# Turning the last tile inside a unit, writing two engines' loops out, and moving one head's meta scores in a two-block kernel

## The reference

```python
for l in range(2):                                   # first block
    h = rmsnorm(x, pre_g[l])
    u_a, v_a, g_a, q, k, v, g_b = split(h @ w_in[l])
    y_a = gmlp(u_a, layernorm(v_a)) * silu(g_a)      # spatial mixing in chunks of 128
    y_b = attention(rope(rmsnorm(q)), rope(rmsnorm(k)), v) * silu(g_b)
    x = x + rmsnorm(concat(y_a, y_b) @ w_out[l], post_g[l])
h = concat(pad, meta, x)                             # second block: 16 meta tokens ahead
sb_q, sb_k, sb_v, sw_q, ... = split(rms_norm(h) @ w_in_2)
o_sb = stick_breaking_attention(sb_q, sb_k, sb_v)    # 8 heads, weights from suffix sums
o_sw = sliding_window_sink_attention(...)            # 16 heads, window of 128
merged = sigmoid(g_sb) * ((o_sb * silu(sb_z)) @ w_branch_sb) + sigmoid(g_sw) * (...)
out = rms_norm(h + merged @ w_out_2)[:, 128:]
```

## Time and profile before

| | |
|---|---|
| Time before, median of 3 runs | 984.11 us (983.71 to 984.31) |
| The profiled execution's own time | 981.8 us |
| Its span, first to last instruction | 980.0 us |
| PE busy | 961.1 us (98%) |
| VectorE busy | 639.5 us (65%) |
| ScalarE busy | 492.6 us (50%) |
| GpSimd busy | 257.1 us (26%) |
| DMA, mean | 82 GB/s |

### The profile page before, as it was taken

One profiled execution on the slowest core, in us unless ns is written; L12 is line 12 of the kernel. 1 busy time (PEld: TensorE's weight loads), 2 busy tenths in 40 slices (PEclk: granted clock), 3 DMA queues, 4 the chain that ended last, 5 costly groups with the idle time before them and its releaser, 6 DMA issues.

```text
span 980.0 us, 13699 instructions
## 1 busy us (share of the span) xinstructions
PE 961.1 (98%) x4922; PEld 812.0 (83%) x4922; DVE 639.5 (65%) x949; ACT 492.6 (50%) x903; POOL 257.1 (26%) x205
## 2 busy tenths in 40 slices
PE   7999999999999999999999999999999999999997
PEld 6988888888888888888787888888888887888885
DVE  5677777937687687846655798599557985312214
ACT  5435665624435655625347777423657983222212
POOL 2216200003126200002342010340325885224231
PEclk9999999999999999999999999999999999999999
DMA  8332201232422301132332111122320112223312
GB/s 289 109 117 71 89 22 44 62 114 87 142 87 86 105 26 44 44 129 82 108 99 77 40 43 44 43 86 87 102 92 1 44 44 81 92 89 105 129 43 86
DMA packets 66791, 80.45 MB, mean 82 GB/s; under 512 B 5520, under 2 KB 50704, under 8 KB 66720
## 3 DMA queue, kind: packets, MB, share of 16 engines
q1 hardware_dynamic: 64816, 76.64, 24.5%
q10 hardware_dynamic: 1904, 2.88, 0.9%
HBM read 77.42 MB, written 2.10 MB: 81 GB/s over the span
## 4 chain that ended last, share of the span: by engine, by line
PE 60%; issue 29%; DVE 4%; POOL 3%; ACT 3%; DMA 1%; POOLq 0%; ACTq 0%; DVEq 0%
PE ps L1944 16%; PE ps L1946 16%; PE ps L1945 16%; PE ps L2001 1%; PE ps L1999 1%; PE ps L2000 1%; PE ps L2322 1%; PE ps L2458 1%; PE ps L2473 1%; DVE pwt L1604 1%; POOL small L561 1%; DMA x<-in_x 1%; PE ps L2486 1%; PE ps L2342 1%; PE ps L2205 1%
## 5 line engine op out<-in xcount | busy, mean ns | idle before, releaser
L606 POOL TENSOR_TENSOR wlo<-raw,whi 128x2048 fp32r<-128x2048 f32 (+1 forms) x22 | 96.3, 4375 | 186.2 <-ACT whi L958 176.8
L1944 PE MATMUL ps<-whi,hhi 128*128 128x512 f32 (+1 forms) x320 | 115.9, 362 | 1.5 <-DVE hlo L1267 0.8
L1946 PE MATMUL ps<-whi,hlo 128*128 128x512 f32 (+1 forms) x320 | 114.5, 358 | 0.0
L1945 PE MATMUL ps<-wlo,hhi 128*128 128x512 f32 (+1 forms) x320 | 114.4, 357 | 0.0
L1944 PE MATMUL ps<-hhi,whi 128*128 128x512 f32 x288 | 113.6, 394 | 0.3 <-ACT sp L1055 0.3
L1946 PE MATMUL ps<-hhi,wlo 128*128 128x512 f32 x288 | 112.3, 390 | 0.0
L1945 PE MATMUL ps<-hlo,whi 128*128 128x512 f32 x288 | 112.3, 390 | 0.0
L958 ACT ACTIVATE whi<-raw 128x2048 fp32r<-128x2048 f32 (+1 forms) x29 | 53.0, 1826 | 84.0 <-PE ps L1946 74.1
L1276 DVE TENSOR_TENSOR wlo<-raw,whi 128x2048 fp32r<-128x2048 f32 (+1 forms) x29 | 63.6, 2193 | 39.4 <-ACT whi L724 38.0
L724 ACT ACTIVATE whi<-raw 128x2048 fp32r<-128x2048 f32 (+1 forms) x29 | 52.2, 1799 | 72.7 <-PE ps L1946 72.7
L1999 PE MATMUL ps<-hhi,whi 128*128 128x512 f32 x192 | 76.9, 400 | 0.0
(11 more groups left out here) (331 smaller groups left out, 2339.9 us busy)
## 6 DMA issues: line engine op xcount, KB each, us to landing
raw<-in_w_in SPq DMA_DIRECT2D x42, 1024.0 KB, 5.3
raw<-in_w_out SPq DMA_DIRECT2D x12, 1024.0 KB, 5.0
raw<-in_w_in SPq DMA_DIRECT2D x10, 512.0 KB, 4.2
raw<-in_w_branch_swa SPq DMA_DIRECT2D x4, 1024.0 KB, 5.3
raw<-in_w_branch_sb SPq DMA_DIRECT2D x4, 512.0 KB, 3.4
x<-in_x ACTq DMA_DIRECT2D x3, 512.0 KB, 6.8
out<-x SPq DMA_DIRECT2D x3, 512.0 KB, 2.6
ws<-in_spatial_w SPq DMA_DIRECT2D x2, 512.0 KB, 6.8
```

The lines of the kernel that those rows point to most:

```text
L606: pool.tensor_tensor(wlo[s][:, 0:n, :], raw[s][:, 0:n, :], whi[s][:, 0:n, :].bitcast(F32), ALU.subtract).then_inc(slab_split, 1)
L1944: pe.matmul(out_ap, lhsT=lhi(k), rhs=rhi(k), start=first and k == 0, stop=False, skip_group_check=True)
L1945: pe.matmul(out_ap, lhsT=lhi(k), rhs=rlo(k), start=False, stop=False, skip_group_check=True)
L1946: m = pe.matmul(out_ap, lhsT=llo(k), rhs=rhi(k), start=False, stop=last and k == n - 1, skip_group_check=True)
```

## The change

Five edits:

- Tile 3 is turned inside unit (0, 2), between its two groups of six products, instead of ahead of it. This holds in both layers and in the second block.
- ScalarE's and VectorE's loops over the two layers become Python loops, so the layers are written out one after the other; PE, GpSimd and SyncE keep their loops.
- At the end of a layer VectorE makes the first half of tile 2's `hlo` ahead of `normalise` of tile 3, the second half behind it.
- In the second block the meta scores of head 1 go behind both gate units, and in round 1 VectorE makes `meta_keys_lo(1)` ahead of `terms_lo(2)`.
- At the end GpSimd adds epsilon to the first half's sum as soon as that is there, and then adds this to the second half's.

```diff
-TILE_AT = {3: 2, 4: 3}
+TILE_AT = {3: 2}
+LAST_TILE_AT = 4
...
             for t in range(NT):
+                if t == 3:
+                    pool.wait_ge(fin_sq, 4)
+                    first = small2[:, 16:17]
+                    pool.tensor_tensor(first, first, eps_tile[:, 0:1], ALU.add).then_inc(last_sum, 1)
+                    pool.wait_ge(last_sum, 1)
                 pool.wait_ge(fin_sq, t + 1 + t // 3)
                 m = small2[:, 8 + t:9 + t]
-                if t == 3:
-                    pool.tensor_tensor(m, m, small2[:, 16:17], ALU.add).then_inc(last_sum, 1)
-                    pool.wait_ge(last_sum, 1)
-                pool.tensor_tensor(m, m, eps_tile[:, 0:1], ALU.add).then_inc(pool_step, 1)
+                pool.tensor_tensor(m, m, small2[:, 16:17] if t == 3 else eps_tile[:, 0:1], ALU.add)\
+                    .then_inc(pool_step, 1)
...
-            with act.Fori(0, DEPTH) as l:
+            for l in range(DEPTH):
...
-            with dve.Fori(0, DEPTH) as l:
+            for l in range(DEPTH):
...
                 normalise(l, 1, 2)
                 post_add(3)
+                transposed_x(l, 1, 2, (0,))
                 normalise(l, 1, 3)
-                transposed_x(l, 1, 2)
+                transposed_x(l, 1, 2, (1,))
...
-                    terms_lo(h + 1)
                     if h == 1:
                         meta_keys_lo(1)
+                    terms_lo(h + 1)
...
-                def by_token_half(i, half, t):
+                def by_token_half(i, half, t, turned_between=None):
...
                     for at_ in (0, 2):
+                        if at_ and turned_between is not None:
+                            x_transposed(l, 0, turned_between)
...
-                    by_token_half(i, i, t)
+                    by_token_half(i, i, t, 3 if n == LAST_TILE_AT else None)
...
             other_scores(0)
-            stick_meta_scores(1)
             gate_unit(0)
             gate_unit(1)
+            stick_meta_scores(1)
```

More of the change, by code:

```diff
@@ L2171, in tokens, with tokens_half @@
                         lambda k: whi[s][:, k, :], lambda k: wlo[s][:, k, :], KT).then_inc(unit_done, 1)
-            def tokens_half(j, half, t):
+            def tokens_half(j, half, t, turned_between=None):
                 s, tt = j % RING, slice(t * P, t * P + P)
@@ L2178, in tokens_half @@
                 for at_ in (0, 2):
+                    if at_ and turned_between is not None:
+                        x_transposed(DEPTH, 0, turned_between)
                     if (j, t) == (0, 0):
@@ L2235, in _ @@
                     m.then_inc(mt_done, 1)
-                tokens_half(j, j, t)
+                tokens_half(j, j, t, 3 if n == LAST_TILE_AT else None)
                 if t == 3:
```

## The result

The changed kernel takes 977.57 us, median of 4 runs (977.45 to 977.75); the kernel before, timed beside it, 983.91 us (983.67 to 984.31). The ratio is 0.9945, with a 95% interval of 0.9933 to 0.9956 (the two medians divide to 0.9936): 6.3 us faster, where 4.2 were forecast.

A forecast was written before the change was run, and what follows sets the result against it. TensorE, busy 961.1 of 980.0 us, was taken as the bound. The terms 1.3 + 0.75 + 1.9 + 0.27 = 4.2 us, off the median of 984.11, gave 979.9 us; range 979.0 to 982.1.

The forecast's parts named there:

- can only close gaps: Whole kernel: no matrix product is removed, so only TensorE's 18.9 us outside its busy time can be won.
- The meta scores, 1.9 us: Second block, head 1: gates fill TensorE's wait for VectorE's low part of `qsb`; 1.9 us won, bounds 0 to 2.2.
- Rival A: Meta scores of the second head: the 1.9 us are given back, 2.3 us remain, 981.8 us; chance 0.12.
- The start of the second layer, 1.3 us: Loops' back edges and turn of tile 3: unit (0,3) starts 1.3 us earlier; bounds 0.6 to 1.4.
- Rival B: Turn inside the unit fails to hide tile 3, or ScalarE and VectorE stall at the layer's start; 981.9 us, chance 0.11.
- The start of the second block, 0.75 us: Same new order without a back edge: unit (0,3) starts 0.75 us earlier; bounds 0.3 to 0.84.
- a slow first step: Start of the second block: TensorE resumes at about 474.95 with its first step 0.1 us longer; 0.2 us lost there.
- The end, 0.27 us: Behind the last product: one of three GpSimd operations is done earlier, so the root and all behind it move 0.27 us.
- The spread: Whole kernel: the forecast's own spread, from the bounds of its terms, given as 979.3 to 980.9 us.
- Rival C: ScalarE and VectorE through the second layer: fetching the second code copy shows; slower from six fetches, up to 989.7 us; chance 0.05.
- the prediction's signs of being wrong: TensorE's idle merely moved to unit (0,3) or the sums, or "issue" on ScalarE or VectorE in the second layer.

## Why the prediction was right in its parts and wrong in its sum

**The step that failed** is the last one: "That execution lies 2.3 us under the median of 984.11, so the forecast is 984.11 - 4.2 = 979.9 us." It took the 2.3 us between the profile and the timed runs for a constant that any version of the kernel carries. They were 1.7 us of half clock (983.87 - 982.2, the medians of the two groups) and chance: the profiled execution lies 0.4 us under the median of the lower group, and the 984.11 of the three runs 0.2 above that of the upper one. With it failed the premise that the change "can only close gaps": it also keeps products from running at half clock, which counts as busy time and which no list of waits shows. The clock falls behind the very stop that the change removes, so the upper group went with the stop: none of 29 runs of six kernels without it (the changed one, the meta scores alone, and the changed one without the turn, with the loops in, with the old end, with TensorE's loop out) and none of 22 with the stop filled or half filled is in an upper group. What was needed stood in the numbers: three times within 0.6 us of one another and a profiled execution 1.9 us under the lowest of them. That does not look like scatter: either every profile reads less, or something was in those three executions and not in the profiled one. A second profile would have told the two apart. And a profile at full clock can't show what a stop costs where the clock falls.

**The meta scores, 1.9 us.** Right: sums of head 1 come 540.20 - 516.78 = 23.42 us behind the last score of head 0, before 543.87 - 518.43 = 25.44, so 2.0 us; alone, the edit gives 2.0 in the lower group. The true term against the runs shown is 3.7, the rest being the clock. Rival A (the gain given back) did not come: the sums of head 0 are 2.2 us sooner and those of head 1 2.0.

**The start of the second layer, 1.3 us.** Right: from the last product of unit (1,1) to unit (0,3) it is 253.68 - 249.83 = 3.85 us, before 254.68 - 249.46 = 5.22, so 1.37. ScalarE's "issue" ahead of tile 3 is gone. Rival B's stall is what the kernel with loops in shows: there the same stretch takes 4.64 us, 0.6 less than before, which is the term's lower bound.

**The start of the second block, 0.75 us.** Right: 5.46 - 4.71 = 0.75, with a slow first step at 473.98 as foreseen. No run has this part alone.

**The end, 0.27 us.** The rows after are one GpSimd step shorter than in the kernel with the old end (0.27 us against 0.53), and the times differ by 0.2: right in the profiles, and within what five runs can tell in the times.

**The spread.** By the prediction's own bounds its ends are 984.11 - 4.7 = 979.4 and 984.11 - 3.1 = 981.0 us, not 979.3 and 980.9; nothing hangs on it.

**Rival C** (the second copy of the code fetched visibly) did not come as a cost: there are 21 packets in place of 29 on that queue, no "issue" on ScalarE at the place it named, and none of TensorE's listed waits from its back edge at 238.16 to 582.48. But one of the prediction's signs of being wrong did come: VectorE shows "issue" in the second layer, ahead of the low part of a slab, in all seven profiles with the loops out, where before the same idle ends with ScalarE's `whi`. After:

```profile
256.68 1.92 ACT L728 ACTIVATE whi<-raw 128x2048 fp32r<-128x2048 f32 x1 [1.57 <-PE ps L1951]
...
259.04 2.29 DVE L1280 TENSOR_TENSOR wlo<-raw,whi 128x2048 fp32r<-128x2048 f32 x1 [3.36 <-issue]
```

Before:

```profile
259.79 2.29 DVE L1276 TENSOR_TENSOR wlo<-raw,whi 128x2048 fp32r<-128x2048 f32 x1 [2.86 <-ACT whi L724]
```

Most of the 3.36 us passes before ScalarE is done (256.68 + 1.92 = 258.60); VectorE starts 0.44 us behind that, before it was 0.12 (257.75 + 1.92 = 259.67 and 259.79). So some 0.3 us on VectorE are new, and TensorE does not wait for them. Whether they are a fetch is not shown, and no view names the 3.34 us of the earlier trace rows a fetch either. The Trainium skill, "Runtime: NRT & Kernel Launch", section "Instruction fetch mechanics", says that in straight code the edges of blocks are mostly hidden; the times agree, those of TensorE's own code written out too (0.5 us less).

**What the sum did not have:** TensorE's own back edge varies by some tenths from execution to execution (a step of 0.54 us in the first profile of before, 0.79 in its second, 0.78 after, 1.10 with loops in), and a stop of TensorE near 777, behind VectorE's "issue" of 0.25 us, is in all six profiles with loops in and in none of the seven with them out. It accounts for 0.3 us of the profiles' 4.3. That code laid out differently moves this stop is argued from those profiles, not shown.

## What to carry to other kernels

When the profiled execution lies outside the scatter of the timed runs, find what the one has and the other lacks before adding the difference to a forecast: it can be a cost with a place, and the change may touch it. A stop of TensorE of 1.95 us cost nearly twice its length here, since the clock fell behind it in some of the executions; look at the granted clock behind each long stop, in more than one profile, and not at waits alone, since a slow product counts as busy. Where such a stop can't be removed, a few useless products in it are worth a trial: here they saved the clock in 22 of 22 runs. Two edits at one place (the loop's back edge and the turn) can each look small alone and be worth more than their sum together, as here (0.9 and 0.5 us, together 2.4).

## What the runs showed of the hardware that was not expected

- One kernel on one core has two times, 1.7 us apart, in a mix of about one to two, by whether the granted clock falls to half behind one stop of 1.95 us. Stops of 0.8 us (ahead of the values at 814 in the first profile of before) and of about 1.0 us (half filled) kept it, and so did one of 1.85 us in one execution; one of 2.83 us lost it and one of 2.02 us kept it in the same execution.
- Useless products made the kernel faster: eight of them, 1.8 us of work, took 1.5 us off the median.
- ScalarE's idle at its loop's back edge was 3.34 to 3.55 us in all six profiles with loops in, though the turn that it waits for began at 250.25 in one and at 251.65 in another; with the loops out it came to tile 3 0.64 us (after) and 0.69 us (loops alone) behind the start of the turn.
- The kernel with written-out loops fetched less on the instruction queue shown, not more: 0.17 MB against 0.24.
